# Hybrid attention and recurrence layer on one core: the attention phase in periods of two blocks instead of one

## Chip, core and metric

One core of one Trainium2 chip. The metric is the device time of one execution in microseconds (us), the median of several runs. PE is the matrix engine, PEld its weight loads, DVE, ACT and POOL the vector, scalar and GpSimd engines, SP the engine that issues the transfers.

## What is computed

One layer over 2048 tokens of width 1024. After RMS norm and a shift and scale, an input projection feeds two branches: attention of 16 query heads of width 64 in 4 groups, each with one key and value head and a window of 128, and a gated recurrence of 8 heads, which the change leaves as it is. The attention part of the reference:

```python
    aq = rope(rms_norm(aq.reshape(B, S, ATTN_HEADS, ATTN_HEAD_DIM), q_norm_w), positions)
    ak = rope(rms_norm(ak.reshape(B, S, ATTN_KV_HEADS, ATTN_HEAD_DIM), k_norm_w), positions)
    ...
    s = jnp.einsum('bnqhgd,bnkhd->bnhgqk', qb, kk,
                   preferred_element_type=jnp.float32) * (hd ** -0.5)
    ...
    m = jnp.maximum(jnp.max(s, axis=-1, keepdims=True), sink)
    p = jnp.exp(s - m)
    denom = jnp.sum(p, axis=-1, keepdims=True) + jnp.exp(sink - m)
    o = jnp.einsum('bnhgqk,bnkhd->bnqhgd', (p / denom).astype(v.dtype), vv)
```

The result, times SiLU of a gate, goes with the recurrence's rows through one output projection.

## The kernel before

The 2048 tokens are worked in two segments (`SEGS`). Each segment has three phases: large projections of values and gates (Strassen products), attention, recurrence. After both comes the output projection. The change touches the attention phase alone, which stands at about 276 to 535 us in the first segment and 1008 to 1267 us in the second.

A segment's attention phase works 32 blocks (`ATT_B`): 4 head groups by 8 blocks of 128 tokens. Every engine runs its own program in an order written out by hand, `att_iter(s, b)`, and semaphores tie them together. So an instruction late on one engine holds back all that stands behind it on that engine. Every projection is a sum of three products of high and low halves of the numbers, at L902, 24 products for one block.

A block j passes these steps, in this order, with the lines of before:

- PE projects q, k and v of the block (L902, into bank 0 or 1). ACT squares them (`sq`, L1488) and copies v (`vv`). DVE sums the squares (`q_ss`, L2096), POOL makes the root in two instructions (`q_var` L2437 and `q_rinv` L2439, 5 numbers in each row), DVE scales (`qn`, L2055), and POOL rotates q and k (L2477 to L2493, eight instructions, the last of them `q_rot` and `k_rot`).
- PE turns q and k (L1012, L1015) into bank 4. ACT and DVE copy them out as high and low halves (L1460, L2063).
- PE makes the scores (L1080), 12 products of 64 rows in concurrent pairs, into banks 2 and 3. DVE masks them and takes the maximum (L2037 to L2046, `neg_m`), ACT takes the exponentials (L1480), DVE the reciprocal of the sum, ACT normalises (L1499).
- PE turns the four heads' weights (L1048, 8 transposes from `sm` into banks 5 and 6), ACT and DVE copy them out (`pT`), PE makes the value products (L1059, 8 instructions with 64 columns of the array each, in pairs, into bank 7), DVE multiplies with the gate (`o_mix`, L2114), SP stores.

In turn b, PE turns q and k of block b-2, projects block b, turns the weights of block b-4, makes values of block b-5 and then scores of block b-2. While this goes on, ACT and DVE also split the weights of the next head group into halves, in four parts of 768 columns (`wq_hi` L1353 on ACT, `wq_lo` L1882 on DVE, from SBUF to SBUF with two inputs from there), one part in each of turns 2 to 5 of eight; in the last group it is the recurrence's first weights, two parts of 1024 columns. On DVE this part stands behind the gate's product `g_q` (L2077), and so beside POOL's rotation.

The root of POOL waits for `ss_ok` (DVE's sum) and the scaling `qn` waits for `rinv_ok`:

```python
                waits = [(ss_ok, S + b + 1)]
                if b >= 1:
                    waits.append((qn_ok, S + b))
                waits_alone(pool, *waits)
                inverse_root(q_rinv, q_var, q_ss, HD, rinv_ok, 2 * (S + b))
```

## Time and profile before

| | |
|---|---|
| median of 3 runs | 1814.87 us (1813.16 to 1815.29) |
| the profiled execution | 1813.45 us, of which its span is 1811.7 us |
| PE busy | 1775.8 us, 98% of the span |
| DVE, ACT, POOL busy | 1293.6, 973.6 and 481.5 us (71%, 54%, 27%) |
| PE in the chain that ended last | 88% of the span |
| granted PE clock | 0.996 over the span, 1.00 inside the attention phase |

The span goes from the first to the last instruction of the program. Rows of the timeline give the start in us from the start of the span, the length, the engine, the line, the operation, what it writes and reads, its shape and how many were merged. PE's instructions overlap: a length is that of the whole pipeline, and what one costs is the distance from start to start.

### The profile page before, as it was taken

Reading aid. Unit: us, or ns where it says so; the run is one execution under the profiler, and the core shown is the slowest. Engines: PE = TensorE matmul, PEld = TensorE weight load, DVE = VectorE, ACT = ScalarE, POOL = GpSimd, SP = SyncE. Lnnn points to the kernel's source line nnn. Section 1 sums busy time; section 2 is a strip of 40 time slices with the busy share of each in tenths; the row PEclk is TensorE's granted clock in tenths of the full one; section 3 lists DMA queues with packets and bytes.
Section 4 is the critical chain, followed back from the end, with each engine's and each line's share of the span. In section 5 each row is a group of like instructions: output and inputs, shape, how many; then the busy total and the mean of one; then the engine's idle time right before and its main releaser. Section 6 shows DMA issues by size and latency. Waiting matters only on the chain.

```text
span 1811.7 us, 28428 instructions
## 1 busy us (share of the span) xinstructions
PE 1775.8 (98%) x9856; PEld 1507.4 (83%) x9856; DVE 1293.6 (71%) x2692; ACT 973.6 (54%) x2127; POOL 481.5 (27%) x825
## 2 busy tenths in 40 slices
PE   6999999999999999999999999999999999999999
PEld 4788888888878888878888888887888888888887
DVE  7966476777767666696646777776786657987987
ACT  5622225777776565552222577877556555343441
POOL 1000026667722222200002567773222220000000
PEclk9999999999999999999999999999999999999999
DMA  9142322221223444344133222121432248278252
GB/s 359 70 163 96 114 105 100 74 71 40 86 68 118 123 136 133 106 168 163 75 123 109 105 75 65 46 86 33 156 127 80 72 145 313 83 250 295 107 180 93
DMA packets 158494, 222.30 MB, mean 123 GB/s; under 512 B 11792, under 2 KB 104336, under 8 KB 150672
## 3 DMA queue, kind: packets, MB, share of 16 engines
q1 hardware_dynamic: 158352, 220.49, 36.0%
q8 instruction: 79, 1.29, 0.3%
q14 instruction: 63, 0.52, 0.1%
HBM read 163.18 MB, written 57.28 MB: 122 GB/s over the span
## 4 chain that ended last, share of the span: by engine, by line
PE 88%; DVE 5%; DMA 2%; issue 2%; POOL 1%; ACT 1%; SPq 0%; DVEq 0%; POOLq 0%; ACTq 0%
PE bank L902 68%; PE bank L1059 3%; PE bank L1048 3%; PE bank L1080 3%; PE bank L1110 2%; PE bank L1128 2%; PE bank L1143 1%; PE bank L1106 1%; PE bank L1012 1%; PE bank L1156 1%; PE bank L1133 1%; DMA o_lower<-mixed_cols 1%; DVE g_lo L1795 1%; DMA ob_raw<-in_w_out 0%; PE bank L1097 0%
## 5 line engine op out<-in xcount | busy, mean ns | idle before, releaser
L902 PE MATMUL bank<-h_hi,w_hi 128*128 128x512 f32 x512 | 205.9, 402 | 0.2
L902 PE MATMUL bank<-h_lo,w_hi 128*128 128x512 f32 x512 | 199.9, 390 | 0.0
L902 PE MATMUL bank<-h_hi,w_lo 128*128 128x512 f32 x512 | 199.6, 390 | 0.0
L902 PE MATMUL bank<-wq_hi,h_hi 128*128 128x384 f32 x512 | 176.9, 346 | 0.5 <-issue 0.5
L902 PE MATMUL bank<-ob_hi,oa_hi 128*128 128x512 f32 x448 | 175.0, 391 | 1.0 <-DVE ua L2232 0.8
L902 PE MATMUL bank<-ob_hi,oa_lo 128*128 128x512 f32 x448 | 174.4, 389 | 0.0
L902 PE MATMUL bank<-ob_lo,oa_hi 128*128 128x512 f32 x448 | 174.3, 389 | 0.0
L902 PE MATMUL bank<-wq_hi,h_lo 128*128 128x384 f32 x512 | 171.9, 336 | 0.0
L902 PE MATMUL bank<-wq_lo,h_hi 128*128 128x384 f32 x512 | 171.1, 334 | 0.0
L1324 ACT ACTIVATE g_hi<-g_raw 128x2048 fp32r<-128x2048 f32 x36 | 69.0, 1916 | 162.4 <-PE bank L902 156.4
L1480 ACT ACTIVATE sm<-sm,neg_m 128x257 f32<-128x257 f32 x256 | 127.4, 504 | 18.0 <-DVE neg_m L2046 18.0
L1795 DVE TENSOR_TENSOR g_lo<-g_raw,g_hi 128x2048 fp32r<-128x2048 f32 x36 | 82.9, 2304 | 59.4 <-ACT g_hi L1324 59.4
L902 PEld LDWEIGHTS bank<-h_lo,w_hi 128*128 128x128 f32 x512 | 96.1, 188 | 20.6
L902 PEld LDWEIGHTS bank<-h_hi,w_hi 128*128 128x128 f32 x512 | 96.3, 188 | 20.3 <-issue 2.4
L2521 POOL TENSOR_TENSOR b_cum<-b_cum,mid_sum 128x256 f32<-128x256 f32 x32 | 20.8, 652 | 346.6 <-DVE mid_sum L2015 346.6
L902 PEld LDWEIGHTS bank<-h_hi,w_lo 128*128 128x128 f32 x512 | 96.3, 188 | 18.5 <-issue 0.5
L1499 ACT ACTIVATE sm<-sm,r_den 128x256 f32<-128x256 f32 x256 | 108.9, 505 | 2.1 <-DVE r_den L2093 2.1
L902 PE MATMUL bank<-g_hi,h_hi 128*128 128x512 f32 x256 | 102.6, 401 | 6.6 <-DVE h_lo L1839 6.3
L902 PE MATMUL bank<-g_lo,h_hi 128*128 128x512 f32 x256 | 101.0, 395 | 0.0
L902 PE MATMUL bank<-g_hi,h_lo 128*128 128x512 f32 x256 | 100.6, 393 | 0.0
L902 PEld LDWEIGHTS bank<-ob_hi,oa_hi 128*128 128x128 f32 x448 | 84.1, 188 | 19.2 <-issue 2.2
L902 PEld LDWEIGHTS bank<-ob_hi,oa_lo 128*128 128x128 f32 x448 | 84.1, 188 | 17.7
(256 smaller groups left out, 4695.8 us busy)
## 6 DMA issues: line engine op xcount, KB each, us to landing
g_raw<-in_w_in SPq DMA_DIRECT2D x24, 1024.0 KB, 6.2
raw<-in_w_in SPq DMA_DIRECT2D x16, 1024.0 KB, 8.1
o_lower<-mixed_cols SPq DMA_DIRECT2D x32, 512.0 KB, 6.7
nat_rows<-u SPq DMA_DIRECT2D x48, 256.0 KB, 2.6
raw<-in_w_in SPq DMA_DIRECT2D x8, 1536.0 KB, 6.5
o_upper<-in_w_out SPq DMA_DIRECT2D x24, 512.0 KB, 9.0
wa<-in_w_ada SPq DMA_DIRECT2D x8, 1024.0 KB, 10.7
g_q<-gate_cols SPq DMA_DIRECT2D x64, 128.0 KB, 2.4
```

Of the source, the lines that this page charges most:

```text
L902: mm = pe.matmul(dst, a, b, start=(first and m == 0), stop=(last and m == 2), **more)
L1012: pe.transpose(bank[4][:, h * P:(h + 1) * P], q_rot[j % 2][:, 2 * h:2 * h + 2, :].rearrange("p a d -> p (a d)"), ident[:])
L1048: mm = pe.transpose(bank[5 + h // 2][:, at:at + P], sm[j % 2][:, h, half * P:(half + 1) * P], ident[:])
L1059: mm = pe.matmul(bank[7][e * HD:(e + 1) * HD, 0:2 * P], vv[:, j % NBLK + half, :], pT[j % 2][:, e:GH:2, half, :], start=(half == 0), stop= ...
L1080: mm = pe.matmul(bank[2 + h % 2][:, (h // 2) * 2 * P:(h // 2 + 1) * 2 * P], tq[j % 2][lo:lo + HD, h // 2, :], tk[lo:lo + HD, k0:k0 + 2, :] ...
L1110: mm = pe.matmul(bank[7][:, tokens(q)], q_dec[b][:, tokens(q)], s_mid[b][:, q, :], start=False, stop=True, skip_group_check=True)
L1128: mm = pe.matmul(bank[2][:, tokens(q)], k_inv[b][:, tokens(q)], q_dec[b][:, tokens(q)], start=True, stop=True)
L1324: act.activation(g_hi[w_slot(n, e)][:], src[:], ACT.Copy).then_inc(whi_ok, 1)
L1480: act.activation(sm[j % 2][:, h, 0:2 * P + 1], sm[j % 2][:, h, 0:2 * P + 1], ACT.Exp, bias=neg_m[j % 2][:, h:h + 1], accum_out=den[j % 2][ ...
L1499: a = act.activation(sm[j % 2][:, h, 0:2 * P], sm[j % 2][:, h, 0:2 * P], ACT.Identity, scale=r_den[j % 2][:, h:h + 1])
L1795: dve.tensor_tensor(g_lo[w_slot(n, e)][:], src[:], g_hi[w_slot(n, e)][:].bitcast(F32), ALU.subtract).then_inc(wlo_ok, 1)
L2521: pool.tensor_tensor(early, early, mid_sum[:].unsqueeze(2).to_broadcast([P, QB, CH]), ALU.subtract).then_inc(mid_ok, 1)
```

## The change

The phase is written in periods of two blocks, `att_pair(s, m)`, 16 periods (`PAIRS`) and three more that fill and empty it. In period m, PE turns q and k of block 2m-2, projects block 2m, projects the first half of block 2m+1, turns q and k of block 2m-1, and goes on with the projection, inside which it turns the weights of block 2m-4; after it the weights of block 2m-3. Then come the values of blocks 2m-5 and 2m-4 together, and the scores of blocks 2m-2 and 2m-1 together. Scores of odd blocks go to banks 5 and 6, which they share with the turned weights; values of odd and even blocks go to the two halves of bank 7. The orders of ACT and DVE follow. The gate product becomes one instruction of 256 columns instead of two of 128. DVE's parts of the weight split stand in slots, `next_weights(s, m, slot)`: in the second, third and fourth of four periods one stands right behind the sum of squares of block 2m (slot 1), and in the fourth one more between the reciprocals (slot 0). SP loads the next group's weights after block 1 of a group instead of block 3. POOL's program is the same. The number of instructions on PE for each block is the same.

```diff
@@ -45,11 +45,13 @@
-LAG = 5
+LAG = 3
...
+PAIRS = ATT_B // 2
+LAST = ATT_B - 1
@@ -468,6 +470,16 @@
+        def score(j, h):
+
+            return bank[(2 if j % 2 == 0 else 5) + h % 2][:, (h // 2) * 2 * P:(h // 2 + 1) * 2 * P]
+
+        def value_bank(j):
+
+            if j == LAST:
+                return bank[2][:, 0:2 * P]
+            return bank[7][:, 0:2 * P] if j % 2 else bank[7][:, 2 * P:4 * P]
@@ -651,7 +663,7 @@
-                    if i == 3 and g + 1 < GROUPS:
+                    if i == 1 and g + 1 < GROUPS:
@@ -987,100 +999,155 @@
...
+            def scores(s, j):
+
+                S = s * ATT_B
+                pe.wait_ge(tcopy_ok, 2 * (S + j + 1))
+                if j == 0:
+                    pe.wait_ge(comb_ok, 20 * GU * (s + 1))
+                if j >= 2 and j % 2 == 0:
+                    pe.wait_ge(masked_ok, (GH + 1) * (S + j - 1))
+                elif j >= 2:
+                    pe.wait_ge(pta_ok, S + j - 1)
+                    pe.wait_ge(ptv_ok, S + j - 1)
...
+            def turn_p(s, j):
+
+                S = s * ATT_B
+                pe.wait_ge(pn_ok, S + j + 1)
+                if j % 2 == 0:
+                    pe.wait_ge(masked_ok, (GH + 1) * (S + j + 2))
+                if j >= 1:
+                    pe.wait_ge(pta_ok, S + j)
+                    pe.wait_ge(ptv_ok, S + j)
...
+            def values(s, j):
+
+                S = s * ATT_B
+                pe.wait_ge(pta_ok, S + j + 1)
+                pe.wait_ge(ptv_ok, S + j + 1)
+                if j < LAST and j >= 1:
+                    pe.wait_ge(omix_ok, S + (j if j % 2 else j - 1))
+                dst = value_bank(j)
...
+            def att_pair(s, m):
+
+                j, p = 2 * m - 2, 2 * m - 4
+                if 2 <= m <= PAIRS:
+                    turn_qk(s, j)
+                if m < PAIRS:
+                    project_block(s, 2 * m, range(KH))
+                    if m == 1:
+                        turn_qk(s, j)
+                    project_block(s, 2 * m, range(KH, KT))
+                    project_block(s, 2 * m + 1, range(KH))
+                    if m >= 1:
+                        turn_qk(s, j + 1)
+                    project_block(s, 2 * m + 1, range(KH, KT - 2))
+                    if m >= 2:
+                        turn_p(s, p)
+                    project_block(s, 2 * m + 1, range(KT - 2, KT))
+                    if m >= 2:
+                        turn_p(s, p + 1)
+                if m == PAIRS:
+                    qkv_free(s, ATT_B)
...
+                if m >= 3:
+                    values(s, p - 1)
+                if 2 <= m <= PAIRS + 1:
+                    values(s, p)
+                if 1 <= m < PAIRS:
+                    scores(s, j)
+                    scores(s, j + 1)
...
@@ -1445,69 +1514,112 @@
...
+            def att_pair(s, m):
+                j, p = 2 * m - 2, 2 * m - 4
+                if m == PAIRS + 1:
+                    decays(s, 0)
+                if 1 <= m <= PAIRS:
+                    turned_hi(s, j)
+                if 2 <= m <= PAIRS:
+                    exps(s, p)
+                if 2 <= m <= PAIRS + 1:
+                    exps(s, p + 1)
+                if m < PAIRS:
+                    squares_and_v(s, 2 * m)
+                if m == PAIRS:
+                    act.wait_ge(krot_ok, (s + 1) * ATT_B)
                     forget_tanh(s, 0)
+                if 2 <= m <= PAIRS:
+                    normalise(s, p)
+                if 2 <= m <= PAIRS + 1:
+                    normalise(s, p + 1)
+                    p_copy(s, p)
+                if 1 <= m <= PAIRS:
+                    turned_hi(s, j + 1)
+                if m < PAIRS:
+                    squares_and_v(s, 2 * m + 1)
+                if m == PAIRS:
                     forget_log(s, 0)
+                if 2 <= m <= PAIRS + 1:
+                    gate_tanh(s, p)
+                    gate_tanh(s, p + 1)
+                if m == PAIRS:
+                    exps(s, LAST - 1)
+                if 2 <= m <= PAIRS + 1:
+                    p_copy(s, p + 1)
+                if m == PAIRS:
+                    normalise(s, LAST - 1)
+                if m < PAIRS:
+                    next_weights(s, m)
...
@@ -2023,97 +2135,143 @@
...
+            def next_weights(s, m, slot):
+                g, at = m // (NBLK // 2), m % (NBLK // 2)
+                part = ((None, None), (None, 0), (None, 1), (2, 3))[at][slot]
+                if part is not None and m < PAIRS:
                     if g + 1 < GROUPS:
                         att_weights_lo(s, g + 1, part)
                     elif part < 2:
                         rec_weights_lo(s, 0, (part,))
+            def att_pair(s, m):
+                j, p = 2 * m - 2, 2 * m - 4
+                if 2 <= m <= PAIRS:
+                    mask_scores(s, p)
+                if 2 <= m <= PAIRS + 1:
+                    mask_scores(s, p + 1)
+                if 1 <= m <= PAIRS:
+                    turned_lo(s, j)
+                if m >= 3:
+                    scale_gate(s, p - 1)
+                if 2 <= m <= PAIRS:
+                    invert_den(s, p)
+                next_weights(s, m, 0)
+                if 2 <= m <= PAIRS + 1:
+                    invert_den(s, p + 1)
+                if m < PAIRS:
+                    sum_squares(s, 2 * m)
+                    next_weights(s, m, 1)
+                    norm_qk(s, 2 * m)
+                if m == 0:
+                    rotate_first(s)
+                if m == PAIRS:
+                    forget_gate(s, 0)
+                    dve.memset(chunk_keep[:], 1.0).then_inc(keep_ok, 1)
+                    dve.wait_ge(keep_ok, s + 1)
+                    dve.memset(chunk_keep[:].rearrange("p (c t) -> p c t", t=CH)[:, :, 0:1], 0.0)
+                if 2 <= m <= PAIRS + 1:
+                    p_copy(s, p)
+                if m == PAIRS:
+                    mask_scores(s, LAST - 1)
+                if 1 <= m <= PAIRS:
+                    turned_lo(s, j + 1)
+                if m < PAIRS:
+                    sum_squares(s, 2 * m + 1)
+                if m == PAIRS:
+                    forget_sums(s, 0)
+                if m == PAIRS + 1:
+                    decay_q(s, 0)
+                    dve.wait_ge(s_ok, (s + 1) * ATT_B)
                     dve.memset(a_T[:], 0.0)
+                if 2 <= m <= PAIRS + 1:
+                    scale_gate(s, p)
+                    p_copy(s, p + 1)
+                if m == PAIRS:
+                    invert_den(s, LAST - 1)
+                if m >= 3:
+                    mix_block(s, p - 1)
+                if 2 <= m <= PAIRS + 1:
+                    mix_block(s, p)
+                if m < PAIRS:
+                    norm_qk(s, 2 * m + 1)
```

PE's queue in the middle of the phase, before: what stands between two projections (bank and `sm`, `pT`, `qT` carry their buffer's number).

```order
L1048 MATMUL bank5<-ident,sm0 128x128 x4
L1048 MATMUL bank6<-ident,sm0 128x128 x4
L1059 MATMUL bank7<-pT1,vv 64x256 x4
...
L1080 MATMUL bank2<-kT_hi,qT_lo0 128x256
L1080 MATMUL bank3<-kT_hi,qT_lo0 128x256
L1012 MATMUL bank4<-ident,q_rot1 128x128 x2
L1015 MATMUL bank4<-ident,k_rot1 128x128
L902 MATMUL bank1<-wq_hi1,h_hi 128x384
```

After, the end of a projection and what follows it; L914, L1025, L1088, L1102 and L1072 are L902, L1012, L1048, L1059 and L1080 of before.

```order
L914 MATMUL bank1<-wq_hi1,h_lo 128x384
L1025 MATMUL bank4<-ident,q_rot1 128x128 x2
...
L914 MATMUL bank1<-wq_hi1,h_lo 128x384
L1088 MATMUL bank5<-ident,sm0 128x128 x4
L1088 MATMUL bank6<-ident,sm0 128x128 x4
...
L914 MATMUL bank1<-wq_hi1,h_lo 128x384
L1088 MATMUL bank5<-ident,sm1 128x128 x4
L1088 MATMUL bank6<-ident,sm1 128x128 x4
L1102 MATMUL bank7<-pT1,vv 64x256 x4
L1102 MATMUL bank7<-pT0,vv 64x256 x4
L1072 MATMUL bank2<-kT_hi,qT_hi0 128x256
```

Of the sixteen weight transposes of two blocks, the eight of the first now stand inside the projection, the other eight behind it, and the value products of two blocks (`pT1`, `pT0`) follow each other, as do the scores of two blocks.

DVE's queue before, from the end of a mask step to the sum of squares; the weight part follows `g_q`.

```order
L2046 SCALAR_TENSOR_TENSOR neg_m0<-row_max,sink_neg 128x4
L2055 TENSOR_TENSOR qn<-bank0,q_rinv 128x320
L2063 TENSOR_TENSOR qT_lo1<-bank4,qT_hi1 128x256
L2067 TENSOR_TENSOR kT_lo<-bank4,kT_hi 128x128
L2077 SCALAR_TENSOR_TENSOR g_q1<-g_t1,g_q1 128x256
L1882 TENSOR_TENSOR wq_lo0<-raw0,wq_hi0 128x768
L2093 RECIPROCAL r_den0<-den0 128x4
L2096 TENSOR_REDUCE q_ss<-sq 128x5
```

After, in a fourth period of four; L1994, L2193, L2165 are L1882, L2096, L2055 of before.

```order
L2182 SCALAR_TENSOR_TENSOR g_q1<-g_t1,g_q1 128x256
L2188 RECIPROCAL r_den0<-den0 128x4
L1994 TENSOR_TENSOR wq_lo0<-raw0,wq_hi0 128x768
L2188 RECIPROCAL r_den1<-den1 128x4
L2193 TENSOR_REDUCE q_ss<-sq 128x5
L1994 TENSOR_TENSOR wq_lo0<-raw0,wq_hi0 128x768
L2165 TENSOR_TENSOR qn<-bank0,q_rinv 128x320
L2201 COPY pT0<-bank6 128x512
```

One weight part moved between the two reciprocals, the other between the sum of squares `q_ss` and the scaling `qn`, that is, to the time at which POOL makes the root out of `q_ss`.

## Rows read from the trace of the kernel before

**Rows 1.** Busy times, 300 to 500 us: PE, PEld, DVE, ACT, POOL; clock, DMA share, GB/s.

```profile
300.00:500.00 200.00, 200.00 (x1477) 177.15 (x1476) 148.82 (x521) 157.74 (x498) 142.57 (x270) 1.00 0.21 64
```

**Rows 2.** Timeline of PE over one block (start, us, what; bracket: idle before).

```profile
406.09 1.03 PE L1048 MATMUL bank<-ident,sm 128*128 128x128 f32 x8
407.06 1.08 PE L1059 MATMUL bank<-pT,vv 128*64 128x256 f32 x8
408.07 0.39 PE L1080 MATMUL bank<-kT_hi,qT_hi 64*128 64x256 f32 x2
408.29 0.28 PE L1080 MATMUL bank<-kT_lo,qT_hi 64*128 64x256 f32 x2
...
408.77 0.28 PE L1080 MATMUL bank<-kT_hi,qT_lo 64*128 64x256 f32 x2
408.98 0.44 PE L1012 MATMUL bank<-ident,q_rot 128*128 128x128 f32 x2
409.25 0.27 PE L1015 MATMUL bank<-ident,k_rot 128*128 128x128 f32 x1
409.28 0.42 PE L902 MATMUL bank<-wq_hi,h_hi 128*128 128x384 f32 x1
...
413.55 0.27 PE L1048 MATMUL bank<-ident,sm 128*128 128x128 f32 x1
```

**Rows 3.** Timeline of PE, 407.50 to 407.53: the second value pair.

```profile
407.32 0.39 PE L1059 MATMUL bank<-pT,vv 128*64 128x256 f32 x2
```

**Rows 4.** Timeline of DVE, the mask step of a block.

```profile
401.69 0.17 DVE L2037 COPY sm<-sink_bc 128x4 f32<-128x4 f32 x1 [0.47 <-issue]
...
403.27 0.16 DVE L2046 SCALAR_TENSOR_TENSOR neg_m<-row_max,sink_neg 128x4 f32<-128x4 f32 x1
```

**Rows 5.** Timeline of ACT, exponentials, squares and normalising of a block.

```profile
403.58 0.51 ACT L1480 ACTIVATE sm<-sm,neg_m 128x257 f32<-128x257 f32 x1
...
404.08 0.51 ACT L1480 ACTIVATE sm<-sm,neg_m 128x257 f32<-128x257 f32 x1
...
406.29 0.44 ACT L1488 ACTIVATE sq<-bank 128x320 f32<-128x320 f32 x1 [0.63 <-PE bank L902]
...
406.73 1.70 ACT L1499 ACTIVATE sm<-sm,r_den 128x256 f32<-128x256 f32 x4
```

**Rows 6.** Timeline of DVE at the start of the phase.

```profile
285.19 0.48 DVE L2096 TENSOR_REDUCE q_ss<-sq 128x5 f32<-128x320 f32 x1
287.34 0.49 DVE L2055 TENSOR_TENSOR qn<-bank,q_rinv 128x320 f32<-128x320 f32 x1 [1.67 <-POOL q_rinv L2439]
287.75 0.41 DVE L2063 TENSOR_TENSOR qT_lo<-bank,qT_hi 128x256 fp32r<-128x256 f32 x1
```

**Rows 7.** Timeline of POOL at the start of the phase.

```profile
285.83 0.20 POOL L2437 TENSOR_SCALAR q_var<-q_ss 128x5 f32<-128x5 f32 x1 [0.24 <-issue]
286.11 1.19 POOL L2439 TENSOR_TENSOR q_rinv<-q_var,minus_half 128x5 f32<-128x5 f32 x1
287.91 0.74 POOL L2477 TENSOR_TENSOR rc<-qn,rot 128x256 f32<-128x256 f32 x1 [0.60 <-DVE qn L2055]
```

**Rows 8.** Timeline of POOL, rotation of a block with no weight split beside it.

```profile
448.77 0.74 POOL L2477 TENSOR_TENSOR rc<-qn,rot 128x256 f32<-128x256 f32 x1 [2.34 <-DVE qn L2055]
...
450.50 0.32 POOL L2483 TENSOR_TENSOR rc<-qn,rot 128x64 f32<-128x64 f32 x1
...
451.89 0.46 POOL L2493 TENSOR_TENSOR k_rot<-rc,rs 128x128 f32<-128x128 f32 x1
```

**Rows 9.** Timeline of DVE, a weight split.

```profile
289.27 1.02 DVE L1882 TENSOR_TENSOR wq_lo<-raw,wq_hi 128x768 fp32r<-128x768 f32 x1 [0.92 <-ACT wq_hi L1353]
```

**Rows 10.** Timeline of POOL beside that split.

```profile
289.44 1.04 POOL L2483 TENSOR_TENSOR rc<-qn,rot 128x64 f32<-128x64 f32 x1
```

**Rows 11.** Waits of PE, whole run (in total, times, longest).

```profile
PE bank L1012 <- POOL q_rot L2491: 1.6, 3, 0.6
...
PE bank L1012 <- DVE q_rot L1996: 1.4, 2, 0.8
```

More of the change, by code:

```diff
@@ new lines, in values @@
+            def values(s, j):
+                S = s * ATT_B
+                pe.wait_ge(pta_ok, S + j + 1)
[3 more added lines that the diff above has]
+                dst = value_bank(j)
+                for half in range(2):
+                    for e in range(2):
+                        mm = pe.matmul(dst[e * HD:(e + 1) * HD, :], vv[:, j % NBLK + half, :],
+                                       pT[j % 2][:, e:GH:2, half, :], start=(half == 0), stop=(half == 1))
+                mm.then_inc(pv_ok, 1)
@@ L1266, in _ @@
                 arrive(pe)
-                for b in range(ATT_B + LAG):
-                    att_iter(s, b)
+                for m in range(PAIRS + LAG):
+                    att_pair(s, m)
                 arrive(pe)
@@ new lines, in exps, with normalise @@
+            def exps(s, j):
+                act.wait_ge(max_ok, s * ATT_B + j + 1)
+                for h in range(GH):
+                    act.activation(sm[j % 2][:, h, 0:2 * P + 1], sm[j % 2][:, h, 0:2 * P + 1], ACT.Exp,
+                                   bias=neg_m[j % 2][:, h:h + 1], accum_out=den[j % 2][:, h:h + 1]).then_inc(exp_ok, 1)
+            def normalise(s, j):
+                act.wait_ge(rden_ok, s * ATT_B + j + 1)
+                for h in range(GH):
+                    a = act.activation(sm[j % 2][:, h, 0:2 * P], sm[j % 2][:, h, 0:2 * P], ACT.Identity,
+                                       scale=r_den[j % 2][:, h:h + 1])
+                a.then_inc(pn_ok, 1)
@@ L1678, in _ @@
                 meet(act, att_phase(s))
-                for b in range(ATT_B + LAG - 1):
-                    att_iter(s, b)
+                for m in range(PAIRS + LAG - 1):
+                    att_pair(s, m)
                 arrive(act)
@@ new lines, in mask_scores @@
+                waits = [(s_ok, S + j + 1)]
+                if j >= 1:
+                    waits.append((max_ok, S + j))
+                if j >= 2:
+                    waits.append((pt_ok, S + j - 1))
+                waits_alone(dve, *waits)
+                sinks_at = slice(j // NBLK * GH, (j // NBLK + 1) * GH)
+                dve.tensor_copy(sm[j % 2][:, :, 2 * P:2 * P + 1], sink_bc[:, sinks_at].unsqueeze(2)).then_inc(masked_ok, 1)
+                mask = masks[:, 0 if j % NBLK == 0 and s == 0 else 1, :]
@@ L2411, in _ @@
                     dve.tensor_copy(kT_lo[:, 0, :], no_key[:])
-                for b in range(ATT_B + LAG):
-                    att_iter(s, b)
+                for m in range(PAIRS + LAG):
+                    att_pair(s, m)
                 arrive(dve)
```

374 lines of the change are left out of this document (154 added, 220 removed).

## The prediction

> **What bounds the kernel now.** I read the busy time of a stretch in the middle of an attention phase first: PE is busy for all 200 us of it, while DVE, ACT and POOL are busy for 149, 158 and 143 us [rows 1]. So PE sets the time, and the others have a quarter of theirs to spare. Then I read PE's timeline over one block for what the 7.46 us from one row of weight turns (406.09) to the next (413.55) are made of [rows 2]. The projection takes 4.27 us (409.28 to 413.55). The other 3.19 us are transposes, value products and score products, and here the reader should compare the distance from start to start with the steady one:
>
> - Eight transposes have length 1.03 and one alone 0.27, so they stand 0.11 apart. They would be over at 406.96; the values start at 407.06: 0.10 more.
> - The second value pair starts 0.26 after the first [rows 3], the others 0.22 apart ((1.08 - 0.26 - 0.39)/2): 0.05 more. Four pairs would end at 407.97, the scores start at 408.07: 0.10 more.
> - The first score pair takes 0.22, the next four 0.12 each: 0.10 more. After the last the transposes start at 408.98 instead of 408.89: 0.09 more. The first two of them take 0.27 instead of 0.22: 0.05 more.
>
> One round through three shapes (whole array, 64 columns, 64 rows) costs 0.49 us, and before it is paid for every block. PE hardly waits for anybody: its waits for turned q in the whole run are 3.0 us, all at the starts of the two phases [rows 11].
>
> **PE's own work after.** Values of two blocks and scores of two blocks stand together, so the 0.49 is paid once for two blocks. By the fill and the end of the pipeline some 15 rounds are saved in each phase, not 16: 15 x 0.49 = 7.4 us. Against it stands one more place for each period at which a projection goes on behind transposes. There the first product starts 0.03 after the last transpose instead of 0.11, but is itself 0.42 long, longer than its successors [rows 2]; I bound this between 0 and 0.1 and take 0.03, 0.5 us for a phase. Transposes behind a projection start in step, and cost only themselves, which they did before. Two blocks are 14.92 us now and 14.46 after, and a phase has 6.9 us less of PE work. The single gate product (256 columns for twice 128) shortens DVE a little, where there is room; SP's earlier load has a whole period to land, before its part is split; neither is on the path. I cost both at nothing.
>
> **The loop that comes in its place.** Before, every block's mask, exponentials and rotation had a turn of its own. After, the orders of three engines form a closed loop, which takes as long as it takes whatever PE does. It runs from the scaling `qn` of an odd block to the `qn` of the next odd one. Behind `qn` on DVE stands the mask of the period (0.41 later [rows 6]); it takes 1.74 [rows 4]; a release costs 0.04 (the end of `q_rinv` at 287.30 to `qn` at 287.34 [rows 6, 7]); on ACT eight exponentials 0.49 apart take 3.95, and the squares of the even block stand behind them, 0.44 [rows 5]; release 0.04, sum 0.48, and 0.16 until POOL starts; the root takes 1.47; release 0.04, `qn` 0.49, 0.08 until POOL rotates [rows 6, 7]; the rotation takes 3.58 (448.77 to 452.35 [rows 8]); then 0.09, and POOL's root for the odd block, 1.47, and 0.04. The sum is 14.52 us. The 3.58 hold 0.2 of waiting beside the gate's product `g_q` (the first three instructions take 1.73, from 448.77 to 450.50 [rows 8]; at the start of the phase, without it, 1.53, from 287.91 to 289.44 [rows 7, 10]), which can hit or miss the rotation, so 14.3 to 14.5. That is PE's 14.46 almost exactly: without more, the loop would just be hidden.
>
> But in three of four periods a weight part now stands between the sum of squares and `qn`. It starts about 0.4 after the sum and POOL's `q_var` about 0.64 after it, so 0.2 into the part. The nearest row: a part starts at 289.27 and takes 1.02 [rows 9]; POOL's instruction of 64 columns, which starts 0.17 into it, takes 1.04 [rows 10] where it takes 0.32 alone [rows 8]. It ends 0.19 after the part does. Before, such a part hit the rotation, which had a second and more to spare. If `q_var` is held the same way, it ends about 1.45 after the sum's start instead of 0.84: the loop is 0.6 longer, 14.9 to 15.1, and I take 15.0. The bounds are 0 (five numbers slip through) and 0.72 (the row).
>
> The Trainium skill's page "SBUF — State Buffer", section "Who interferes with whom", says that a DVE instruction with two inputs in SBUF and a GpSimd instruction that reads SBUF exclude each other, and the later one fully blocks. It speaks against this change: by it the whole wait is paid even for five numbers, and the result is my forecast; without it, it would be the first rival. The row of 64 columns agrees; no row shows it for five.
>
> Late next is `normalise` of the period's first block, which PE needs 8.2 us into its period (turn 0.36, projections 4.27 + 2.13, turn 0.36, a quarter 1.07). Behind the waiting transposes stand the last products of the projection, and with them all of the next period, but nothing of the loop: it is not fed by PE. So PE pays the difference, 15.0 - 14.46 = 0.54, in each such period.
>
> **The sum for one phase.** PE's work: -6.9. Steady periods with a part in that slot, apart from the first ones: 8 (two or three for each group of four periods), 8 x 0.54 = +4.3. The start: the turn of block 1 waits some 0.9. POOL needs 1.47 + 0.04 + 0.49 + 0.08 + 3.5 + 0.09 = 5.7 for a block, and PE has 4.4 of work from the turn of block 1 to that of block 2 (turn 0.36, half a projection 2.13, scores of two blocks 1.9): 1.3. The weights of block 0 are normalised 9.9 after the turn of block 2 (root 1.6, scaling 0.4, mask 1.74, exponentials 4.0, squares and v 0.44, normalising 1.7 [rows 5]), while PE gets there in 8.2: 1.7. In the next period PE has only one block of values, 13.6 of work against the loop's 15.0: 1.3. Together 5.2 to 5.4 in place of 1.8 now (the 1.5 of [rows 11] and 0.3 for turned k): +3.5. The end: scores of the last block wait for copies out of the banks that they now share with the turned weights, 0.9; a wait for `o_mix` of 0.7 goes: +0.3 with small ones. Sum: -6.9 + 4.3 + 3.5 + 0.3 = +1.2 us, +2.4 for both phases. The profiled execution took 1813.45, which gives 1815.9; it lies 1.4 under the median of 1814.87, on which it gives 1817.3. I predict **1817 us**: no change that can be told. About 0.2%, 3.6 us, is what a measurement of this kernel can tell.
>
> **Rivals.**
>
> - POOL's short instructions aren't held. The loop is 14.3 to 14.5, hidden or nearly so. Then a phase gets -6.9, +0.3 at the end, +0.5 for a loop of 14.5, and +2.3 at the start: -3.8, and the time is 1807. For it: nothing in the trace shows a held instruction of five numbers; against it: the row with 64 columns waits to the very end of the part. Chance 0.24, with all cases in which the loop is under 14.73, from where the gain is over 3.6 us (22 periods x 0.27 = 6 from my sum).
> - The loop is longer, and the kernel slower. POOL's rotation now lies beside the masks, whose ends, `neg_m`, have two inputs in SBUF as the parts have; one wait for a rotation step is up to 0.42 (rows of 0.32 to 0.74 for a step [rows 8]), and the recurrence's two parts have 1024 columns instead of 768. With 0.4 more in 22 periods this gives +8.8 and 1826. It decides from a loop of 15.06 on, so very little is needed. For it: everything I left out adds and nothing subtracts. Against it: measured releases already stand in the sum. Chance 0.32.
> - The rounds aren't saved, because the gaps belong to each block's products and not to the change of shape. Then PE's work stays at 14.92 or above, the loop is mostly hidden under it, and the starts cost 3 us each: 1821. For it: no row shows two blocks' values in a row. Against it: the three gaps stand at the changes of shape alone, and inside a group the distances are steady. Chance 0.04.
>
> **The numbers.** My forecast has 0.40, and its own range is 1813 to 1820. Faster 0.24 is the first rival; slower 0.36 the other two. The range that leaves out no more than 2 in 10 goes from near the first rival to the second: 1805 to 1826.
>
> **What the profile after would show.** PE: value instructions merged by 16, no gap between the two blocks, 0.49 us for each period instead of each block: wrong if a period without any wait isn't near 14.46. POOL: `q_var` of even blocks 0.8 us long in three of four periods, 0.20 in the fourth: if it is 0.20 everywhere, the step on the blocking is wrong. PE should wait for `normalise` (`sm`), 0.3 to 0.6 in those periods, and DVE's `qn` for POOL. If PE waits for something else for more than 3 us in total, a loop that I haven't seen decides; if the starts cost less than 1.8 a phase, that term is wrong.

## The result, and the profile after

| | median | against the kernel before |
|---|---|---|
| before | 1814.99 us | |
| changed | 1832.05 us (1830.68 to 1833.61, 4 runs) | 1.0101 [1.0088, 1.0114], 1% slower |

The change costs 17 us between the medians and 20 between the two profiled executions; the forecast was 1817, and its range ended at 1826. The profiled execution took 1833.61 us, with a span of 1831.8.

The head of the changed kernel's page (busy us, share of the span, instructions):

```profile
## 1 busy us (share of the span) xinstructions
PE 1774.5 (97%) x9856; PEld 1507.7 (82%) x9856; DVE 1271.7 (69%) x2628; ACT 967.7 (53%) x2127; POOL 469.6 (26%) x825
```

PE is busy for 1.3 us less than before, in a span that is 20 us longer. So the loss isn't more work for PE: it is waiting and, as the clock below shows, some time at half the clock. The same stretch as [rows 1], and PE's waits in the whole run, which answer to [rows 11]:

```profile
300.00:500.00 200.00, 196.62 (x1450) 174.83 (x1450) 139.10 (x502) 153.81 (x496) 135.81 (x268) 1.00 0.21 63
```

```profile
engine line waited for: us in total, times, longest us
...
PE bank L1072 <- ACT pT L1571: 7.1, 2, 3.6
...
PE bank L1212 <- ACT k_nat L1720: 5.9, 2, 3.6
PE bank L1088 <- ACT sm L1546: 5.4, 8, 1.9
```

The longer ones that are left out here stand outside the attention phases. The wait at L1072 is new, and the one for `k_nat` was 1.4 us in the kernel before. Neither is in the middle of the phase: L1072 are the scores of the last block, L1212 is the recurrence's first state product. In the kernel before, PE's waits from 500 to 560 us were these:

```profile
PE bank L1059 <- DVE o_mix L2114: 0.7, 1, 0.7
PE bank L1143 <- ACT k_nat L1608: 0.7, 1, 0.7
PE bank L1110 <- DVE state L2165: 0.4, 1, 0.4
```

To see where the time goes I cut each phase at four events of PE: its first projection, the turned k of block 6, the turned k of block 30 (so that 12 periods lie between), and the recurrence's first projection after the last values. The last column goes from there to DVE's 41st `s_end`, where the recurrence runs evenly. Microseconds, first phase / second phase:

| | start | 12 periods | end | recurrence's first part |
|---|---|---|---|---|
| before | 51.10 / 51.34 | 179.04 / 179.04 | 28.87 / 28.87 | 169.74 / 164.87 |
| changed | 55.00 / 53.86 | 179.47 / 179.87 | 33.11 / 34.45 | 173.69 / 166.19 |
| difference | +3.9 / +2.5 | +0.4 / +0.8 | +4.2 / +5.6 | +3.9 / +1.3 |
| forecast | +2.1 | -1.2 | +0.3 | 0 |

(The forecast's -6.9 of PE work is spread here as 3 periods of -0.46 at the start and 12 behind them; its other terms stand where it put them.) The periods missed the forecast by 1.6 and 2.0 us for a phase, the start by 1.8 and 0.4. The end and what follows it hold 15 of the 22.8 us that the table adds up to; the rest, to the 20 us between the spans, was gained outside the phases, 1.4 us of it ahead of the first. The start differs from execution to execution: in the profiles of e1, e2, e5 and e6 below, which leave its program as it is, it took 53.3 to 53.6 us in the first phase and 53.7 to 55.1 in the second.

**The periods.** PE's timeline at three places of one period that starts at 373.98 and ends at 388.99 (start, length, what, how many merged):

```profile
382.29 1.09 PE L1088 MATMUL bank<-ident,sm 128*128 128x128 f32 x8
383.14 0.42 PE L914 MATMUL bank<-wq_hi,h_hi 128*128 128x384 f32 x1
...
384.50 1.07 PE L1088 MATMUL bank<-ident,sm 128*128 128x128 f32 x8
385.49 1.95 PE L1102 MATMUL bank<-pT,vv 128*64 128x256 f32 x16
...
388.99 0.33 PE L1025 MATMUL bank<-ident,q_rot 128*128 128x128 f32 x1
```

Sixteen value instructions stand in one row, as foreseen. The period is 15.02 us, and PE pays the difference to its own 14.54 (e3) in waits at the two groups of turns, as foreseen too: the first group starts 0.45 us behind the start of the last product (381.84) instead of 0.17, the second 0.41 behind the one at 384.09. The view counts only 0.1 of each as idle, since the product's length overlaps the rest. A part in slot 1 shows in the period behind it, through the masks: of 18 such periods among the 24, 16 take 14.93 to 15.13 us, and the two behind the first of the recurrence's two larger parts 15.29 and 15.61. The six others take 14.63 to 14.90. On POOL two short and two held `q_var` follow each other (min, median, max in ns):

```profile
L2595 POOL TENSOR_SCALAR q_var<-q_ss x4: 198/484/771, 410.8 to 432.2; 128x5 f32<-128x5 f32 x4
```

**The end.** The chain of waits of the changed kernel, 521 to 553 us (start, length, what):

```profile
522.27 0.17 ACT kT_hi L1525
...
522.45 1.28 ACT L1504
...
523.75 0.72 ACT f_r L1504
...
524.49 1.28 ACT L1533
...
526.50 1.97 ACT sm L1539 x8
528.47 0.49 ACT pT L1571
...
529.05 0.98 PE bank L1072 x12
530.03 4.55 PE bank L914 x12
...
541.45 1.52 DMA mixed_cols<-o_mix
542.98 4.65 issue
547.62 0.64 ACT o_sq L1706
...
548.90 2.35 DVE w_lo L2002 x2
551.25 0.41 DVE f_r L2115
...
551.68 0.72 ACT f_r L1504
552.41 0.49 ACT k_nat L1720
```

The two pieces of 1.28 us without a name are loads of ACT's function tables, around the logarithm of the gate (`forget_log`). They existed before too, 69 in the whole run, before and after. But now the logarithm stands ahead of the exponentials of block 30, and these ahead of the copy `pT` of block 29, which frees the bank for the scores of block 31. The scores wait 3.56 us. The last values come late and in one heap, block 31's `o_mix` waits for a store of block 29, its own store waits its turn, and only then do the engines meet for the recurrence: the 4.65 of "issue". Behind that meeting ACT needs DVE's weight parts and `f_r` before it comes to `k_nat`.

After each of the three waits of 3.6 us PE's clock is lower. Windows of the changed kernel; the third number from the right is the granted clock, 0.5 of it being 1.2 GHz and 1.0 2.4 GHz:

```profile
520.00:525.00 5.00, 5.00 (x39) 3.97 (x39) 3.33 (x14) 3.56 (x6) 0.00 (x0) 1.00 0.00 0
525.00:529.00 4.00, 0.49 (x6) 0.03 (x2) 2.73 (x7) 3.99 (x13) 0.61 (x1) 1.00 0.00 0
531.00:534.00 3.00, 3.00 (x10) 2.35 (x9) 1.16 (x6) 2.77 (x10) 1.58 (x1) 0.59 0.25 72
...
553.00:557.00 4.00, 4.00 (x16) 3.35 (x17) 2.49 (x5) 3.19 (x7) 1.21 (x2) 0.62 0.96 402
...
1273.00:1277.00 4.00, 4.00 (x10) 3.13 (x11) 2.46 (x11) 2.59 (x9) 1.28 (x1) 0.50 0.22 59
```

Products of 512 columns stand 0.43 apart at half the clock (530.47, 530.90, 531.32) instead of 0.23: eight of them, 1.6 us. At the end of the second phase the clock was at half from 1271 to 1277 us, and that end is 34.45 us long instead of 33.11; in e3 and e4, whose end is written the same, it took 33.07 to 33.13 in all four phases. So 1.3 us of the 5.6 came from the clock of this one execution.

### The profile page after: what moved, and what is told of

It reads as the page before. It is cut to its first block, busy times and chain, and to the rows that moved or that the text cites. A ratio compares the mean times of both kernels' runs of the same rounds, so it can differ in the third digit from the quotient of the medians.

```text
span 1831.8 us, 28394 instructions
## 1 busy us (share of the span) xinstructions
PE 1774.5 (97%) x9856; PEld 1507.7 (82%) x9856; DVE 1271.7 (69%) x2628; ACT 967.7 (53%) x2127; POOL 469.6 (26%) x825
## 4 chain that ended last, share of the span: by engine, by line
PE 74%; ACT 8%; DVE 7%; issue 5%; POOL 3%; DMA 2%; SPq 0%; DVEq 0%; POOLq 0%; ACTq 0%
PE bank L914 58%; ACT sm L1539 4%; PE bank L1088 3%; PE bank L1102 3%; PE bank L1072 2%; DVE sm L2151 2%; ACT sm L1546 1%; PE bank L1177 1%; PE bank L1212 1%; PE bank L1197 1%; PE bank L1173 1%; POOL q_rinv L2597 1%; DMA raw<-in_w_in 1%; PE bank L1225 1%; PE bank L1202 1%
## 5 line engine op out<-in xcount | busy, mean ns | idle before, releaser
L914 PE MATMUL bank<-h_hi,w_hi 128*128 128x512 f32 x512 | 208.9, 408 | 0.2
L914 PE MATMUL bank<-h_hi,w_lo 128*128 128x512 f32 x512 | 202.0, 395 | 0.0
L914 PE MATMUL bank<-h_lo,w_hi 128*128 128x512 f32 x512 | 201.6, 394 | 0.0
L914 PE MATMUL bank<-wq_hi,h_hi 128*128 128x384 f32 x512 | 180.2, 352 | 0.5 <-issue 0.5
L914 PE MATMUL bank<-ob_hi,oa_hi 128*128 128x512 f32 x448 | 174.9, 390 | 0.2 <-DVE ob_lo L2347 0.2
L914 PE MATMUL bank<-ob_hi,oa_lo 128*128 128x512 f32 x448 | 174.4, 389 | 0.0
L914 PE MATMUL bank<-ob_lo,oa_hi 128*128 128x512 f32 x448 | 174.3, 389 | 0.0
L914 PE MATMUL bank<-wq_hi,h_lo 128*128 128x384 f32 x512 | 172.6, 337 | 0.0
L914 PE MATMUL bank<-wq_lo,h_hi 128*128 128x384 f32 x512 | 172.1, 336 | 0.0
L914 PEld LDWEIGHTS bank<-h_lo,w_hi 128*128 128x128 f32 x512 | 97.6, 191 | 21.2
L914 PEld LDWEIGHTS bank<-h_hi,w_hi 128*128 128x128 f32 x512 | 97.5, 190 | 20.4 <-issue 1.8
L914 PEld LDWEIGHTS bank<-h_hi,w_lo 128*128 128x128 f32 x512 | 97.8, 191 | 18.7 <-issue 0.5
L914 PE MATMUL bank<-g_hi,h_hi 128*128 128x512 f32 x256 | 101.9, 398 | 7.2 <-DVE h_lo L1951 6.6
L914 PE MATMUL bank<-g_hi,h_lo 128*128 128x512 f32 x256 | 100.4, 392 | 0.0
L914 PE MATMUL bank<-g_lo,h_hi 128*128 128x512 f32 x256 | 100.4, 392 | 0.0
L914 PEld LDWEIGHTS bank<-ob_hi,oa_hi 128*128 128x128 f32 x448 | 84.1, 188 | 18.5 <-issue 1.0
L914 PEld LDWEIGHTS bank<-ob_hi,oa_lo 128*128 128x128 f32 x448 | 84.1, 188 | 17.4
```

Source lines behind the costliest of these rows:

```text
L914: mm = pe.matmul(dst, a, b, start=(first and m == 0), stop=(last and m == 2), **more)
```

## The experiments

Theory A: the end is what the forecast missed, and its cause is the logarithm with its table loads in the middle of the last blocks' softmax, then the late meeting. Theory B (the forecast's own): the weight part holds `q_var` and lengthens the loop in the periods. The rivals stand in each expectation. Ratios are to the kernel before, measured beside each; cuts in the edits are marked with dots.

**e1: the copies of block 29 ahead of the logarithm.** On ACT, and likewise on DVE ahead of `forget_sums`:

```diff
                 if m == PAIRS:
+                    p_copy(s, p + 1)
                     forget_log(s, 0)
...
-                if 2 <= m <= PAIRS + 1:
+                if 2 <= m <= PAIRS + 1 and m != PAIRS:
                     p_copy(s, p + 1)
```

> Changed kernel with one thing moved, on ACT and DVE: the two copies of the turned weights of block 29 stand ahead of the gate's logarithm (ACT) and of its sums (DVE) in the last full period. Theory (what hurts is the logarithm with its two function table loads, 1.28 us each, standing in the middle of the last blocks' softmax: all behind it is late, whichever comes first): the 3.56 us wait of PE's last scores goes to under 0.5, but the exponentials of block 30 now end some 2.5 us later and the turns of block 30 wait about 3 us instead; total within 3 us of the changed kernel's 1832, so 1829 to 1834. Rival (only the copies' place hurts): both waits gone, PE's half clock after them too, about 5 us less in each phase, 1822.

1835.86 us, 1.0123 [1.0108, 1.0138], a little above the expectation's 1829 to 1834. The wait for the bank went, and a longer one came for the turned weights of block 30, whose exponentials now start at 529.69 instead of 526.41. PE's waits, 500 to 560 us:

```profile
PE bank L1088 <- ACT sm L1546: 4.3, 1, 4.3
PE bank L1212 <- ACT k_nat L1721: 3.5, 1, 3.5
```

So it isn't the copy's place alone: whatever stands behind the logarithm is late.

**e2: the logarithm, sums and decays behind all of attention.**

```diff
-                if m == PAIRS:
-                    forget_log(s, 0)
...
+                if m == PAIRS + 1:
+                    forget_log(s, 0)
+                    decays(s, 0)
...
+                if m == PAIRS + 2:
+                    forget_sums(s, 0)
+                    decay_q(s, 0)
```

> Changed kernel with the gate's logarithm, sums and decays of the first quad moved behind all of attention's work (ACT and DVE), so that no function table load stands between the exponentials of blocks 30 and 31. Theory: the 3.56 us wait before the last scores and the half clock behind it (about 1.6 us) go, the recurrence starts about 5 us earlier in each phase; the wait for k_nat at its start stays near 3.5 us. Total 1832 - 10 = 1822, range 1819 to 1825. Rival (the tail is bound by something else, as the last values and stores): under 4 us in total, 1828 or more.

1835.37 us, 1.0121 [1.0106, 1.0136]: the expectation was wrong, and its rival right in effect. PE's waits at the end of attention went down to 1.4 us, and then:

```profile
PE bank L914 <- DVE q_dec L2133: 5.2, 1, 5.2
```

The recurrence's second projection writes bank 1, which `q_dec` must have read, and `q_dec` needs the decays. I had looked at its first consumer in the products, not at the bank. The logarithm has a due time on both sides.

**e5: the logarithm in ACT's gap.** ACT sat idle for 2.6 us ahead of `p_copy(28)`; the logarithm goes there, the sums on DVE behind the copy of block 29, the decays behind the copy of block 30, and the copy of 29 ahead of the exponentials of 30.

```diff
                     normalise(s, p + 1)
+                if m == PAIRS:
+                    forget_log(s, 0)
+                if 2 <= m <= PAIRS + 1:
                     p_copy(s, p)
+                if m == PAIRS + 1:
+                    decays(s, 0)
...
```

> Changed kernel with the last full period's order altered on ACT and DVE: the logarithm of the first quad stands in ACT's idle 2.6 us ahead of the copy of block 28's turned weights, the sums on DVE behind the copy of block 29, the exponentials of block 30 behind that copy, the decays behind the copy of block 30, so that everything the recurrence needs is there in time (in e2 it wasn't: 5.24 us of wait for q_dec). Theory (the wait for the last scores is due to where the logarithm and its table loads stand): waits of 3.56 and the half clock behind them go, some 1.2 us of new waits for the normalised weights of blocks 30 and 31 come, the recurrence starts 4 us earlier in each phase, its own waits for k_nat stay: 1824, range 1822 to 1827. Rival (the loss moves once more into another wait, as in e1 and e2): 1830 or more.

1825.80 us, 1.0068 [1.0051, 1.0084]. ACT's timeline of e5 there:

```profile
516.57 1.28 ACT L1504 ACT_TABLE_LOAD   x1
517.87 0.72 ACT L1504 ACTIVATE f_r<-f_r,head_par 128x512 f32<-128x512 f32 x1
519.20 0.60 ACT L1571 ACTIVATE pT<-bank 128x512 f32<-128x512 f32 x1 [0.60 <-PE bank L1088]
519.69 0.38 ACT L1523 ACTIVATE qT_hi<-bank 128x256 fp32r<-128x256 f32 x1
519.95 0.28 ACT L1525 ACTIVATE kT_hi<-bank 128x128 fp32r<-128x128 f32 x1
520.25 1.28 ACT L1533 ACT_TABLE_LOAD   x1
```

The same instructions and the same loads, but in time in which ACT had nothing else to do. The end stage went from 33.11 and 34.45 to 29.99 in both phases, and the granted clock of 500 to 545 us from 0.96 to 1.00. That settles the first half of theory A: 3.1 and 4.5 us a phase, 7.6 in all (1.3 of it the longer half clock of the second phase), where the medians' ratios differ by 0.0033 or 6 us.

**e6: `k_nat` ahead of the second quad's logarithm.**

```diff
-                    if t < REC_T:
+                    if 1 < t < REC_T:
                         forget_log(s, t)
...
+                    if t == 1:
+                        forget_log(s, t)
```

> As e5, and in the recurrence's first step ACT copies k_nat ahead of the second quad's logarithm instead of behind it. Theory (k_nat is ready for copying some 3 us before the logarithm, which waits for the meeting of the engines, for two weight parts and for DVE): PE's wait of 3.6 and 2.2 us for k_nat goes with the half clock behind it in the first phase, and the logarithm is no later: 3 to 5 us under e5 in all, 1820. Rival (the next wait, for k_inv and q_dec of the second quad, takes its place): within 1 us of e5.

1826.36 us, 1.0069 [1.0051, 1.0087], no gain: the rival. The wait of 2.9 us for `k_nat` became one of 3.5 for the next thing that the meeting makes late:

```profile
PE bank L1177 <- DVE state L2324: 3.5, 1, 3.5
```

**e3: the weight part out of the loop.** It goes from behind the sum of squares (slot 1) to between the reciprocals (slot 0), where POOL has nothing short to do.

```diff
-                part = ((None, None), (None, 0), (None, 1), (2, 3))[at][slot]
-                if part is not None and m < PAIRS:
+                for part in (((), ()), ((0,), ()), ((1,), ()), ((2, 3), ()))[at][slot] if m < PAIRS else ():
```

> Changed kernel with the weight parts of DVE moved from between the sum of squares and the scaling of the even block to the place before the second reciprocal of the softmax sum, where POOL has no short instruction on the loop. Theory (POOL's q_var of 5 columns is held by the part and lengthens the closed loop from 14.6 to 15.0): q_var 0.20 us everywhere, periods 14.6 instead of 15.0, 8 or 9 periods x 0.4 = 3.5 us less in each phase, total 1825, range 1823 to 1827. Rival (the part costs nothing, the loop is 15.0 for another reason): 1832, periods stay at 15.0.

1823.59 us, 1.0058 [1.0043, 1.0073], as the theory said. POOL's `q_var` is 0.20 us everywhere (ns, 64 of them):

```profile
L2594 POOL TENSOR_SCALAR q_var<-q_ss x64: 197/198/203, 281.8 to 1238.6; 128x5 f32<-128x5 f32 x64
```

In the changed kernel 22 of 64 are held, 18 of them to 0.77, 4 to 1.04. The 12 periods take 174.87 and 175.44 us instead of 179.47 and 179.87; most are 14.54, without any wait of PE. That is 4.6 and 4.4 us a phase, 9 in all; the ratios differ by 0.0043 or 8 us. Theory B holds, in size too.

**e11: the same hold in the kernel before.** Each weight part right behind the block's sum of squares.

> Kernel before with one thing moved on DVE: each weight part stands right behind the block's sum of squares instead of two short instructions ahead of it, so that POOL's q_var meets it as in the changed kernel. Theory (the hold is real wherever the part stands there, but costs only where the loop has no room, and before the loop had it): q_var 0.77 in the blocks with a part, no change of time, ratio 0.999 to 1.001. Rival (the hold costs by itself): 26 blocks x 0.57 = 15 us in each phase, or a good part of it.

1813.11 us, 0.9998 [0.9989, 1.0008]. `q_var` is held here as well, 12 times at 0.77 to 0.79 us and twice at 1.05, and all periods from the third on are 14.92 as before. That is 14 times for 28 parts (the expectation's 26 for a phase was a miscount): beside the other 14 parts POOL is still rotating (`k_rot` takes 1.17 to 1.45 us there instead of 0.46), and it comes to `q_var` when the part is over. The rival would have priced 14 holds at 8 us, and the interval ends at 1.5. Only the phase's second period was 1.4 us longer in the profiled execution, where PE waits for POOL's rotation, 1.27 us at 296.83.

**e4 and e8: which loop is it?** e4 gives the saved change of shapes back, with values and scores in turn:

```diff
                 if m >= 3:
                     values(s, p - 1)
+                if 1 <= m < PAIRS:
+                    scores(s, j)
                 if 2 <= m <= PAIRS + 1:
                     values(s, p)
                 if 1 <= m < PAIRS:
-                    scores(s, j)
                     scores(s, j + 1)
```

> Changed kernel with PE's values and scores in turn again (values, scores, values, scores): the saved change of shapes is given back, 0.49 us for each period. Theory (the loop over DVE, ACT and POOL of 15.0 sets the period, PE's own work is 14.46): PE's work becomes 14.95, hidden in the 8 or 9 periods of 15.0, paid with 0.3 in the periods of 14.6; 1 to 2 us more in each phase, total 1835, range 1833 to 1837. Rival (PE's work sets the period): 14 x 0.49 = 6.9 us more in each phase, 1846.

1843.58 us, 1.0171 [1.0154, 1.0188], between theory and rival; most periods are 15.25 to 15.36. DVE shows what I had overlooked (changed kernel first, then e4):

```profile
387.49 0.76 DVE L2210 SCALAR_TENSOR_TENSOR o_mix<-bank,g_q 128x256 f32<-128x256 f32 x2
388.97 0.49 DVE L2165 TENSOR_TENSOR qn<-bank,q_rinv 128x320 f32<-128x320 f32 x1 [0.72 <-POOL q_rinv L2597]
```

```profile
403.05 0.75 DVE L2211 SCALAR_TENSOR_TENSOR o_mix<-bank,g_q 128x256 f32<-128x256 f32 x2 [1.16 <-PE bank L1102]
403.72 0.48 DVE L2166 TENSOR_TENSOR qn<-bank,q_rinv 128x320 f32<-128x320 f32 x1
```

The loop's `qn` stands behind two `o_mix`, which wait for PE's second values. It had 0.72 us of room; e4 brings the values 1.0 later and so the loop 0.3: 15.02 + 0.3 = 15.3. PE's own extra is 0.34 (from the first value to the turn of q, 3.84 us against 3.50), so this run can't tell the two. e8 moves the mixes behind `qn`:

```diff
+                if m < PAIRS:
+                    norm_qk(s, 2 * m + 1)
                 if m >= 3:
                     mix_block(s, p - 1)
                 if 2 <= m <= PAIRS + 1:
                     mix_block(s, p)
-                if m < PAIRS:
-                    norm_qk(s, 2 * m + 1)
```

> As e4 (values and scores in turn, one change of shapes more), but DVE scales the odd block ahead of the two mixes, so that the loop over DVE, ACT and POOL no longer stands behind PE's second values (in e4 qn of the odd block waited for a mix that waited for them). Theory (e4 cost so much because its edit fed the loop from PE): periods with a part go from e4's 15.35 to 15.0 to 15.1, the total to 1834 to 1836. Rival (PE's work is the bound there too, with 0.34 more for the change of shapes and 0.48 that each late normalise costs): periods stay at 15.3, total 1842.

1857.81 us, 1.0243 [1.0227, 1.0258], far outside both. DVE in e8:

```profile
408.48 0.49 DVE L2166 TENSOR_TENSOR qn<-bank,q_rinv 128x320 f32<-128x320 f32 x1 [1.10 <-POOL q_rinv L2598]
408.89 0.74 DVE L2211 SCALAR_TENSOR_TENSOR o_mix<-bank,g_q 128x256 f32<-128x256 f32 x2
409.55 0.26 DVE L2149 COPY sm<-sink_bc 128x4 f32<-128x4 f32 x1
```

The mixes now stand inside the loop, between `qn` and the mask, which is 0.7 us later for it; the periods went to 16.02, and those without a part in front of them to 15.53 to 15.80. 0.7 us of work, moved a few instructions down on an engine that is busy for 70% of the time, made each period 0.7 longer than in e4, with PE's instructions in the same order. So both expectations failed, and the second failure shows what the first was to show: in these periods the loop over DVE, ACT and POOL sets the length, not PE.

**e9: e3 and e5 together.**

> e5 and e3 together: the weight parts out of the loop and the logarithm in ACT's gap at the end, nothing else. Theory (two independent losses that add): the ratio of 1.0101 of the changed kernel less 0.0043 (e3) less 0.0033 (e5), 1.0025, 1818; the starts and the ends of the phases keep 5 us each over the kernel before, and the steady periods of 14.54 against 14.92 give back 8. Rival: the end's waits return since the blocks come earlier, over 1823.

1816.58 us, 1.0022 [1.0012, 1.0031], where the two gains added give 1.0025. They add.

**e7 and e10: towards a version that beats both.** e7 is e3, e5 and e6, with block 29's values behind the scores of block 31, its mix first on DVE, and SP's store of a group's last keys one block earlier.

> e6 and e3 together (weight parts out of the loop, worth 8 us there), and two more of the end: values of block 29 right behind the scores of block 31 and its mix first on DVE, the stores of the group's last keys one block earlier on SP, so that the last store doesn't wait and the engines meet 2 to 3 us earlier. Theory (the losses are independent and add): 1820 - 8 - 1 = 1811, range 1808 to 1815, not slower than the kernel before. Rival (PE's clock or another wait takes it back): over 1816.

1813.28 us, 0.9995 [0.9986, 1.0005], within the expectation. The two waits left in the first phase: 2.15 for `state` (as in e6) and 1.05 for the mix of block 28, in front of the values that I had moved. e10 takes both out: `k_nat` goes back behind the logarithm, as in the changed kernel, and the values of block 29 stand between the turns. The weight part of the second period moves to the third.

```diff
                     turn_p(s, p)
+                    values(s, p - 1)
                     project_f(s, 0, 1, range(KH, KT))
...
```

> e7 without its k_nat ahead of the logarithm, with the values of block 29 behind the turns of block 30 instead of behind the scores of block 31, and with no weight part in the second period of a phase (two in the third instead). Theory (in e7 the early k_nat only let the second quad's logarithm begin 1.9 us later, which PE paid at its next outputs, 2.15 and clock; the values cost 1.05 of wait where they stood): per phase 1.2 + 0.7 + 0.8 us under e7, 1813 - 5 = 1808, range 1806 to 1812. Rival (the recurrence's first steps wait in any order, since they are bound by the meeting of the engines): within 2 us of e7, 1811 to 1814.

1808.76 us, 0.9975 [0.9965, 0.9985], as the theory said: 0.25% faster than the kernel before and 1.3% faster than the changed one. In e10 PE isn't idle in the middle, the clock stays at 1.00, and the recurrence starts as in the kernel before (windows 300 to 500, 500 to 545 and 545 to 560 us):

```profile
300.00:500.00 200.00, 197.67 (x1483) 176.93 (x1482) 146.53 (x500) 160.15 (x512) 132.68 (x274) 1.00 0.21 63
500.00:545.00 45.00, 42.85 (x265) 33.53 (x264) 28.71 (x88) 34.53 (x83) 8.51 (x15) 1.00 0.30 104
545.00:560.00 15.00, 14.56 (x85) 12.65 (x84) 12.99 (x32) 8.39 (x19) 3.79 (x6) 1.00 0.18 51
```

(The 2.3 us that PE lacks in the first of them are two waits at the start, 1.92 and 0.41; from 320 to 500 it has none.) Its stages, first and second phase: start 52.07 / 54.27, 12 periods 175.06 / 175.59, end 29.86 / 29.85, recurrence 169.76 / 164.86. In e9 the last were 172.21 / 166.01. So the late meeting cost 2.5 and 1.2 us, and with the mix and the stores in time it costs nothing: the second half of theory A. e10 differs from e9 in several orders at once (values, mix, stores, sums), and no run shows what each of them is worth.

## Why the prediction was wrong

Right were the loop, its sum and what it costs. The forecast said 15.0 us with a weight part and got 14.93 to 15.13 in 16 of 18 such periods; it said that `q_var` is held until the part's end and ends 0.6 late, and it was 0.57. The rule that it drew on (the Trainium skill, "SBUF — State Buffer", section "Who interferes with whom") agrees with e3 and e11: with five numbers the whole wait is paid. The loop's closure was told too simply, as "it is not fed by PE": e4 shows the link over `o_mix`, which has 0.72 us of room as the kernel stands.

A little off was PE's own work: 14.54 where nothing waits (e3) instead of 14.46, so 0.38 instead of 0.46 for a period, some 1 us a phase. The sum also counted 8 periods with a part in slot 1; behind the first ones there are 9 (and its first rival uses 22 for both phases, which counts the first ones in), and the periods without a part weren't 14.46 but 14.63 to 14.90. Together the 12 periods were 1.6 and 2.0 us a phase over the forecast. The start was 3.9 and 2.5 us dearer instead of 2.1. In the first phase part of it is PE's clock, which no term of the sum had: right after a wait of 1.5 us its row is

```profile
298.00:302.00 4.00, 4.00 (x16) 4.00 (x15) 2.61 (x15) 2.42 (x6) 3.38 (x7) 0.58 0.02 4
```

and 11 products of 384 columns stand 0.32 apart instead of 0.17 there, 1.6 us. It belongs to this execution: e5 and e6, whose start is written the same, have the same wait of 1.5 us there, with no half clock behind it.

None of the three rivals came true: the loop was 15.0 as forecast, neither 14.5 nor 15.4, and the rounds were saved. The kernel was slower than even the second rival said, for another reason. That rival's 0.42 for a held rotation step was a misreading: the 0.32 and the 0.74 of [rows 8] are instructions of 64 and of 256 columns, and their difference is size, not a wait.

The step that failed is the one-line term "The end: scores of the last block wait for copies out of the banks that they now share with the turned weights, 0.9; a wait for `o_mix` of 0.7 goes: +0.3". The wait itself was named rightly, with the wrong price: 3.56 us instead of 0.9, in both phases. I had priced the copy from the moment at which PE's transposes are done, and not followed ACT's own order ahead of it: a table load, the logarithm, a table load, two gates and four exponentials, 5.9 us from 522.45 to 528.38. Four things followed: half the clock, which cost 1.6 us, the late last values, the late meeting, and `k_nat` behind it. The forecast ended at the last values; the recurrence's first steps were no term at all. End and recurrence together were forecast at +0.3 for a phase and measured +8.2 and +6.9; e5 and e10 take back 3.1 and 4.5 of the end, and 3.9 and 1.3 of the recurrence. What remains there is 1.0 us a phase.

The forecast's own test had asked for this ("If PE waits for something else for more than 3 us in total, a loop that I haven't seen decides"): it was 13 us, for `pT` and `k_nat`, of which 1.4 had been there before. What decided was no loop, but the order at the phase's end. In e10 the start is still 1.0 and 2.9 us dearer than in the kernel before. Its trace shows where: PE's waits for `sm`, `q_rot` and `kT_lo` there add up to 3.3 and 4.3 us, against 1.7 and 2.0 before, and in the second phase the granted clock is 0.57 from 1021 to 1025 us, after a wait of 1.9. What stays open is why the wait for `kT_lo` comes in one execution and not in another (1.4 us in the first phase of the changed kernel, none in its second), and what decides whether the clock falls.

## What to carry to other kernels

Where a loop's period changes, price its fill and its end with the same care as the middle: write down, for the engine that is waited for, everything that stands in its order ahead of the awaited instruction, table loads too. Work that is off the path (a logarithm for the next phase, a weight part) has a due time on both sides, and the gap where it is free must be looked up again after each reordering: here the logarithm with its two table loads cost 3 to 5 us a phase in one place, 5 in another, and almost nothing in the third. And a phase isn't over with its last product: look at what the meeting behind it waits for.

## What the hardware showed that I had not expected

- A change between the logarithm's function table and that of tanh costs ACT 1.28 us each way and nothing more: the copy `kT_hi` ends at 522.43, the logarithm starts at 523.75. The Trainium skill, "ScalarE activation tables: per-element evaluation and per-set limits", section "What a function is on this engine", gives 1283 ns, and this trace agrees, with 1.28 us for each of its 69 loads. The Trainium skill, "ScalarE: Activation LUTs", section "What ACT_TABLE_LOAD costs", adds a drain of some 1.4 us, which isn't seen here, so the measurement decides. A plain copy needs no load: in e5 three copies stand between the logarithm and the load back.
- PE fell to half its clock after waits of 1.5 us (298 us), 3.6 (529), 3.6 (553) and 3.6 (1271), though it worked without a pause behind them: 0.58 from 298 to 302, 0.50 from 1273 to 1277. But a wait of 1.9 us in e10's first phase left the clock at 1.00, and one of 1.9 in its second phase was followed by 0.57 (1021 to 1025 us); in e9 the clock stayed at 1.00 even after 3.3 us (543 to 550 us). So the price of a wait isn't its length alone, and its length doesn't tell whether the clock falls: the wait for the last scores cost 3.56 and 1.6 more.
- An instruction of POOL with five numbers takes 0.77 us instead of 0.20 when it meets a DVE instruction of two SBUF inputs, 1.04 with the larger part, in the changed kernel; at the same place on DVE in e11 it is 0.77 to 0.79 and 1.05. In the changed kernel it ends 0.06 us after the DVE instruction does.
